# Attention B of a fused encoder block: 64-column values products in pairs of array halves, row sums by ones products

## The reference

```python
def mla_attention(c_q, c_kv, k_rope, pos, g_cq, g_ckv, w_uq, w_ukv, g_q, g_k):
    q = (rms_norm(c_q, g_cq) @ w_uq).reshape(Bn, S, B_HEADS, B_QK_DIM)      # 8 heads of 96
    kv = (rms_norm(c_kv, g_ckv) @ w_ukv).reshape(Bn, S, B_HEADS, B_NOPE_DIM + B_V_DIM)   # 64 + 64
    ...
    def block(args):
        qi, i = args
        q_chunk = (i * Q_BLOCK + jnp.arange(Q_BLOCK)) // CHUNK              # chunks of 64
        s = jnp.einsum('bqhd,bkhd->bhqk', qi, k).astype(jnp.float32) * scale
        s = jnp.where(key_chunk[None, :] <= q_chunk[:, None], s, -jnp.inf)
        p = jax.nn.softmax(s, axis=-1).astype(v.dtype)
        return jnp.einsum('bhqk,bkhd->bqhd', p, v)
...
merged = gt[:, :, 0] * (y_a @ w_branch_a[l]) + gt[:, :, 1] * (y_b @ w_branch_b[l])
x = x + merged @ w_out[l]
```

## Time and profile before

| | |
|---|---|
| median of 3 runs | 1389.64 us (1389.06 to 1390.81) |
| the profiled execution | 1389.89 us |
| its span | 1388.1 us |
| TensorE busy | 1363.3 us, 98% |
| VectorE busy | 813.6 us, 59% |
| GpSimd busy | 760.2 us, 55% |
| ScalarE busy | 407.4 us, 29% |
| attention B, first slot to last | 172.20 us |

### The profile page before, as it was taken

How to read it: one execution, slowest core, us unless ns; L and a number is a source line. 1 busy time by engine, 2 the same in 40 slices (tenths; PEclk the granted TensorE clock), 3 DMA queues, 4 the chain that set the end, 5 groups by cost and what they waited for, 6 DMA issues and landing times.

```text
span 1388.1 us, 17597 instructions
## 1 busy us (share of the span) xinstructions
PE 1363.3 (98%) x6644; PEld 1117.4 (80%) x6644; DVE 813.6 (59%) x1422; ACT 407.4 (29%) x857; POOL 760.2 (55%) x618
## 2 busy tenths in 40 slices
PE   8999999999999999999999999999999999999998
PEld 8999887668867766888887888888888888888887
DVE  5401725643577762455256667677667777666776
ACT  5113235642355654000033212221221221221121
POOL 2341924445384520354308666668766667866697
PEclk9999999999999999999999999999999999999999
DMA  7120231211120002735101112211111221111113
GB/s 238 41 61 16 86 97 61 65 62 46 41 46 16 9 16 62 246 93 208 33 26 51 53 39 61 61 50 42 54 53 46 61 62 38 54 54 51 48 46 122
DMA packets 102885, 90.82 MB, mean 65 GB/s; under 512 B 21905, under 2 KB 84881, under 8 KB 102801
## 3 DMA queue, kind: packets, MB, share of 16 engines
q1 hardware_dynamic: 102656, 89.17, 21.2%
q10 hardware_dynamic: 144, 0.52, 0.1%
HBM read 76.99 MB, written 12.62 MB: 65 GB/s over the span
## 4 chain that ended last, share of the span: by engine, by line
PE 88%; POOL 4%; DVE 3%; DMA 2%; issue 1%; ACT 1%; ACTq 0%; POOLq 0%; DVEq 0%
PE PS L1452 76%; PE PS L1651 3%; PE PS L1459 2%; PE PS L1826 1%; PE PS L1546 1%; PE PS L1548 1%; DMA r_row<-r_store 1%; PE PS L1631 1%; PE PS L1615 1%; PE PS L1632 1%; PE PS L1633 1%; POOL gw_lo L928 1%; POOL scA L991 1%; POOL b_rstd L879 1%; PE PS L1568 1%
## 5 line engine op out<-in xcount | busy, mean ns | idle before, releaser
L2229 DVE TENSOR_TENSOR xr<-PS,xr 128x512 f32<-128x512 f32 x240 | 161.6, 684 | 80.5 <-PE PS L1452 80.5
L2229 DVE TENSOR_TENSOR sum<-PS,sum 128x512 f32<-128x512 f32 x168 | 114.2, 687 | 90.8 <-PE PS L1452 90.8
L1452 PE MATMUL PS<-w_hi,u_hi 128*128 128x512 f32 x420 | 163.6, 390 | 1.0 <-DVE u_lo L2233 1.0
L1452 PE MATMUL PS<-w_lo,u_hi 128*128 128x512 f32 x420 | 163.4, 389 | 0.0
L1452 PE MATMUL PS<-w_hi,u_lo 128*128 128x512 f32 x420 | 163.4, 389 | 0.0
L1058 POOL TENSOR_TENSOR w_lo<-w_raw,w_hi 128x512 fp32r<-128x512 f32 x109 | 156.0, 1431 | 9.1
L1452 PE MATMUL PS<-mT_hi,w_hi 128*128 128x512 f32 x512 | 160.4, 389 | 0.0
L1452 PE MATMUL PS<-mT_hi,w_lo 128*128 128x512 f32 x512 | 160.2, 389 | 0.0
L1452 PE MATMUL PS<-mT_lo,w_hi 128*128 128x512 f32 x512 | 160.2, 389 | 0.0
L1387 ACT ACTIVATE relu_t<-PS 128x512 f32<-128x512 f32 x64 | 38.3, 599 | 296.1 <-PE PS L1452 293.2
L870 POOL TENSOR_SCALAR w_hi<-w_raw 128x1024 fp32r<-128x1024 f32 x32 | 38.7, 1209 | 156.0 <-DMA w_raw<-in_w_ff 156.0
(11 more groups left out here) (237 smaller groups left out, 2961.0 us busy)
## 6 DMA issues: line engine op xcount, KB each, us to landing
w_raw<-in_w_ff SPq DMA_DIRECT2D x32, 512.0 KB, 4.1
w_raw<-in_w_ff SPq DMA_DIRECT2D x64, 256.0 KB, 2.6
g_raw<-in_w_in SPq DMA_DIRECT2D x16, 512.0 KB, 3.9
gate_store<-gate SPq DMA_DIRECT2D x16, 512.0 KB, 2.6
x_in<-in_x SPq DMA_DIRECT2D x8, 512.0 KB, 10.3
gate_a<-gate_store SPq DMA_DIRECT2D x8, 512.0 KB, 7.6
gate_b<-gate_store SPq DMA_DIRECT2D x8, 512.0 KB, 4.7
raw<-in_w_out SPq DMA_DIRECT2D x8, 512.0 KB, 3.6
```

Source lines behind the costliest of these rows:

```text
L1452: ins = pe.matmul(o, st, cut(mv), start=first and n == 0, stop=last and n == 2)
L2229: dve.tensor_tensor(out, part, out, ALU.add).then_inc(acc_done, 1)
```

## The change

**Values.** Tiles are taken in groups of four: `values_group(j)` stands in slot 4j + 5, in the place where one tile's product stood. A head has three groups: part 0 (triangle of the first half), part 1 (full tiles), part 2 (triangle of the second half). `vB` has only the 64 value columns. In each group some tiles go to the head's own 64 rows of bank 5 or 6 (`head_rows`), the others to the other 64 rows (`other_rows`): in part 1 tiles 1 and 3 to the own ones, in the triangles tiles 1 and 2. ScalarE copies the other rows to `y_raw` (`y_out`), VectorE adds the own rows from PSUM (`y_add`). `p_set` has 3 x 4 tiles, `y_raw` four tiles of full width.

**Sums.** The sums of a head come from four tiles: `p_sum[0]` or `p_sum[3]` (the first triangle added up by GpSimd, `sums_first`), `p_sum[1]` and `p_sum[2]` (two full tiles each, added by VectorE, `full_add`), and `p_set[2][0]` (the second triangle, by GpSimd in place, `sums_last`). Four products with a weight of 32 columns of ones (`sums(h)`) put them in rows 0, 32, 64 and 96 of bank 6, in slot 7 of the next head; for head 7 in bank 7, behind branch 0. ScalarE copies the bank (`sums_out`), four DMAs move the rows (`sum_move`), VectorE adds three of them and takes both reciprocals, and store, two spreads, `y_norm`, `y_high` and `y_low` follow for both halves at once, `y_norm` 31 and 32 slots behind the head's first.

**Order elsewhere.** `yA_lanes` moves to heads 5 and 6, `branch_splits` 0 to 3 to heads 6 and 7, `branch_load` 0 to 3 from head 1 to head 5. New waits: a part 1 group waits for `sums_out` of the previous head (`s_read`), exp of a new set of four for the group, the additions or the ones products that read it.

```diff
-        p_diag = [place(f"p_diag{i}", 40 + 2 * i, [P, HALF]) for i in range(Q_BLOCK)]
-        p_full = [place(f"p_full{i}", 48 + 2 * i, [P, HALF]) for i in range(P_RING)]
-        y_raw = [place(f"y_raw{i}", 58 + 2 * i, [P, HALF]) for i in range(2)]
+        p_set = [[place(f"p_set{g}_{i}", 40 + 8 * g + 2 * i, [P, HALF]) for i in range(Q_BLOCK)] for g in range(3)]
+        y_raw = [place(f"y_raw{j}", (92, 132, 201.75, 144.75)[j], [P, S]) for j in range(4)]
...
-            def sum_move(u):
-                sp.wait_ge(y_raw_ready, u + 1)
-                sp.dma_start(b_sum[:, u % 2, :], sum_row(u).rearrange("o (p t) -> o p t", t=Q_BLOCK)
-                             ).then_inc(sum_landed[u % 2], 16)
+            def sum_move(h):
+                sp.wait_ge(s_read, h + 1)
+                if h:
+                    sp.wait_ge(rsum_b_ready, h)
+                for part in range(4):
+                    sp.dma_start(b_sum[:, part, :], s_raw[32 * part:32 * part + 1, :].rearrange(
+                        "o (p t) -> o p t", t=Q_BLOCK)).then_inc(sum_landed, 16)
...
+                if h >= 2:
+                    reciprocal_store(h - 2)
                 if more:
-                    nmax_move(h + 1, 0, 1, 2)
+                    nmax_move(h + 1, 0, 1)
+                if h >= 2:
+                    reciprocal_spread(h - 2)
+                if more:
+                    nmax_move(h + 1, 2, 3, 4, 5, 6)
                 if h:
-                    sum_move(2 * h - 1)
...
+                    sum_move(h - 1)
                 if more:
                     nmax_move(h + 1, 7)
...
             for d in range(3):
                 fetch_a(d)
-            sum_move(BLOCKS - 1)
-            reciprocal_store(BLOCKS - 1)
-            reciprocal_spread(BLOCKS - 1)
+            reciprocal_store(B_HEADS - 2)
+            reciprocal_spread(B_HEADS - 2)
+            sum_move(B_HEADS - 1)
+            reciprocal_store(B_HEADS - 1)
+            reciprocal_spread(B_HEADS - 1)
             fetch_a(3)
...
+            def sums_first(h):
+                p, d = p_set[0], first_sum(h)
+                pool.wait_ge(p_ready, HEAD_SLOTS * h + Q_BLOCK)
+                if h >= 2:
+                    pool.wait_ge(s_done, h - 1)
+                pool.tensor_scalar(d[:, 0:P], p[0][:, 0:P], 1.0, 1.0, ALU.mult, ALU.mult).then_inc(sum_step, 1)
+                pool.tensor_tensor(d[:, P:], p[0][:, P:], p[1][:, P:], ALU.add).then_inc(sum_step, 1)
+                for i in (2, 3):
+                    add_step(h, i, d[:, i * P:], d[:, i * P:], p[i][:, i * P:])
...
+            for h in range(1, B_HEADS):
+                sums_last(h - 1)
+                sums_first(h)
+                if h in (1, 3):
+                    chain(h + 3)
+                    chain(h + 4)
...
             y_out(BLOCKS - 1)
+            y_high(BLOCKS - 4)
+            y_high(BLOCKS - 3)
+            sums_out(B_HEADS - 1)
             y_high(BLOCKS - 2)
             y_high(BLOCKS - 1)
...
+            def values_group(j):
+
+                h, part = j // 3, j % 3
+                half = min(part, 1)
                 u, g = 2 * h + half, h // B_GROUP
...
+                pe.wait_ge(p_ready, Q_BLOCK * (j + 1))
+                if part < 2 and u >= 2:
+                    pe.wait_ge(y_added, u - 1)
+                if part == 1 and h:
+                    pe.wait_ge(s_read, h)
...
+                for i in range(Q_BLOCK):
+                    own = (i % 2, i in (1, 2))[part != 1]
+                    c0 = P * i if part != 1 else 0
+                    rows = head_rows(h) if own else other_rows(h)
+                    ins = pe.matmul(PS[rows, 5 + half, c0:HALF], vB[g % 3][:, i + Q_BLOCK * (part == 2), h % B_GROUP, :],
+                                    p_set[part][i][:, c0:HALF], start=part < 2 and i < 2, stop=part != 1 and i >= 2)
+                ins.then_inc(group_done, 1)
+
+            def sums(h):
+
+                bank = sums_bank(h)
+                pe.wait_ge(sum_step, SUM_STEPS * (h + 1))
+                pe.wait_ge(full_added, 2 * (h + 1))
...
+                for i, p in enumerate((first_sum(h), p_sum[1], p_sum[2], p_set[2][0])):
+                    ins = pe.matmul(PS[32 * i:32 * i + 32, bank, :], ones_w[:, :], p[:, :], start=True, stop=True)
+                ins.then_inc(s_done, 1)
...
-                if t >= 2:
-                    values_t(t - 2)
+                if t > Q_BLOCK and t % Q_BLOCK == 1:
+                    values_group(t // Q_BLOCK - 1)
                 a = chunk_at(t)
                 if a is not None:
                     approx(a)
+                if t > HEAD_SLOTS and t % HEAD_SLOTS == SUM_AT:
+                    sums(t // HEAD_SLOTS - 1)
...
+            def full_add(h, i):
+                p = p_set[1]
+                dve.wait_ge(p_ready, HEAD_SLOTS * h + 2 * Q_BLOCK)
+                if h:
+                    dve.wait_ge(s_done, h)
+                dve.tensor_tensor(p_sum[1 + i][:, :], p[2 * i][:, :], p[2 * i + 1][:, :], ALU.add).then_inc(full_added, 1)
...
+            def y_add(u):
...
+                c = 0 if half else P
+                y = y_raw[h // 2][head_rows(h), y_cols(half, c)]
+                dve.wait_ge(y_copied, u + 1)
+                dve.tensor_tensor(y, PS[head_rows(h), 5 + half, c:HALF], y, ALU.add).then_inc(y_added, 1)
...
+            y_add(BLOCKS - 1)
+            sum_reciprocal(B_HEADS - 2)
+            y_norm(BLOCKS - 4)
+            y_norm(BLOCKS - 3)
+            y_low(BLOCKS - 4)
+            y_low(BLOCKS - 3)
+            sum_reciprocal(B_HEADS - 1)
             y_norm(BLOCKS - 2)
-            sum_reciprocal(BLOCKS - 1)
+            y_norm(BLOCKS - 1)
             y_low(BLOCKS - 2)
-            y_norm(BLOCKS - 1)
             y_low(BLOCKS - 1)
```

286 lines of the change are left out of this document (159 added, 127 removed).

## The result

The changed kernel takes 1421.16 us as the median of 4 runs (1417.82 to 1423.16), against 1389.87 before: 1.022 times as long, 95% interval 1.0208 to 1.0232. That is 31 us slower, far outside the range of 1384 to 1400. The profiled execution took 1423.11 us. Executions of the changed kernel differ among themselves as their granted clock does: the one of 1417.82 us shows 0.992 over its whole span, those of 1423.1 show 0.986, the kernel before 0.999.

The account below looks back on a forecast made before the run. TensorE, busy 166.15 of attention B's 172.20 us, was taken as the bound over most of it. Stage -4.5 and end +7.6 make +3.1; 1389.89 + 3.1 - 0.25 is about 1393 us, range 1384 to 1400.

Parts of the forecast that it names:

- Side by side, and the shape: TensorE in attention B: array halves run concurrently, values -31.1, sums +6.9, changes of shape +9.3, in all -14.9 us.
- Rival D: Column halves don't run side by side because both write one bank; 1425 us, chance 0.04.
- No term below is a term of the clock: Granted clock of 1.00 in attention B's windows, so the forecast included no clock term.
- The new waits: Each head's full group waits for ScalarE's copy of the previous sums, 0.5 to 1.2 us per head.
- Lanes and branch splits at 0: On GpSimd, lanes and branch splits move from one idle time to another, costing 0 us.
- VectorE and GpSimd in heads 2 and 4: VectorE busy 20.4 to 21.1 us; GpSimd's gapless chain delays ones products 1.1 to 1.5 us each; gain at most 1.
- Rival E: GpSimd and VectorE additions of SBUF tiles hold each other up; stage +3, end +9, 1401.6 us, chance 0.09.
- The row-max transfer: SP's four sum moves precede the last row-max transfer; second-half scores in fast heads wait 0.5 to 1 us.
- The end: Behind attention B, a longer sum chain and late weights delay branch 4, +7.6 us, bounds +4 and +9.5.
- The spreads of head 7: At the end, transfers spreading head 7's reciprocals, taken at 5.2 us and landed by T + 25.1.
- head 6's store: At the end, store issued at T + 2.1 behind three gate transfers, landed about T + 7.
- 10.4 are held back: Part of TensorE's -14.9 us not reaching the stage, which was forecast to gain only 4.5.

Follow-up runs that it names:

- before_with_pauses: The kernel before, with TensorE made to wait three times for dummy GpSimd operations in heads 6 and 7; 1396.49 us.
- copy_first: The changed kernel with ScalarE's copy of the previous head's sums directly behind exp in slot 8; 1410.75 us.
- norm_early: The changed kernel with y_norm, y_high and y_low two slots earlier, the copy of the sums unmoved; 1422.70 us.
- pairs: copy_first with two values products in every odd slot instead of four in every fourth; 1421.54 us.
- end_order: copy_first with head 7's sums copied before head 6's roundings and branch B's first weight load ahead of head 7's store and spreads; 1403.22 us.
- small_additions: The changed kernel with VectorE's two full-tile additions and their ones products on 64 of 512 columns, most second-half sums incomplete; 1413.80 us.

## Why the prediction was wrong

**Side by side, and the shape: right.** TensorE's work was to fall to 166.2 - 14.9 = 151.3 us; without the clock's share it is 152.4. The switch costs the 0.24 us read from the earlier trace rows. Rival D is out.

**"No term below is a term of the clock": the step that failed.** The stage was to gain 4.5 us and lost 25.0, and 15.5 of the difference are a term that the sum did not have. It was read from windows of the kernel before, in which the clock was 1.00 because TensorE never paused long: 0.16 us at the earlier trace rows, 6 us idle in the whole stage, 1.1 at most at once. A change that takes work from the engine that bounds makes pauses, and these have a price that no row of before showed. In its place stand 15.5 us. That pauses are what brings them is shown by before_with_pauses (3.5 us of clock for a pause of 3.04) and fits copy_first (5.2). The clock's share doesn't follow the sum of idle time, though: norm_early has less idle time than the changed kernel and a larger share (20.4), pairs has 6 us less than copy_first and 18.6.

**The new waits: the second step that failed; right mechanism, mis-sized.** The wait for the copy of the sums was put at 0.5 to 1.2 us a head; it was 2.0 on average and 3.6 at most. The sum took exp, y_high and the copy by their durations, as if ScalarE could start each at once. But y_high waits for y_norm, and VectorE comes late to that (heads 2 to 4) or stands there for a row that waits for SP's queue (heads 5 and 7); the reads of preparations and y_out stand ahead of the copy as well. Copying ahead of all but exp gave 10.4 us, a slot earlier still 4.3 to 5.7.

**Lanes and branch splits at 0: wrong in part.** The branch splits cost GpSimd nothing that shows, as said, but their four loads, moved to head 5, stand 2.24 us ahead of the store of the reciprocals on SP, and the store takes 5.5 us beside them instead of 1.6: this is how the longest pause of the stage begins. I had counted the splits and not the queue. No run has the loads elsewhere, so that what they cost is not shown.

**VectorE and GpSimd in heads 2 and 4: not the bound.** VectorE was to be busy 20.4 to 21.1 us there; it was 17.75 and 19.59 of 23.90 and 26.88. In head 2 one y_low and one kT_lo fall into the next head's window, and a y_norm takes 0.67 us instead of the 0.89 of before. It is late slot by slot all the same: row maxima make TensorE wait 6.4 us (0.3 before). GpSimd's chain costs 3.5 (2.0 before); the ones products wait for its last addition once, 0.8 us, where 1.1 to 1.5 were forecast in each of heads 2 and 4. Rival E named a contention that isn't in the added work to speak of: the additions took 0.68 on average (see below for another).

**The row-max transfer:** forecast 0.5 to 1 us for the fast heads, measured once, 2.4 us, in head 7.

**The end: right, mis-sized.** +7.6 was forecast, +4.8 measured, by the wait that was named, for the weights of branch 4. The spreads of head 7, taken at 5.2 us, landed 3.7 us after their issue; everything ahead was 1.5 to 2 us early too. One step came out by luck: head 6's store, issued at T + 2.1, was taken as landed at T + 7 beside a row of 7.1 us, which would give T + 9.2; SP goes on behind it at T + 6.3 (578.44). With end_order nearly all of it goes.

**The balance.** Forecast: -14.9, of which 10.4 are held back, and +7.6. Measured: -13.8 of work, +23.2 of idle time, +15.5 of clock, +4.8 at the end. The 10.4 held back would have been 17.9 with every wait at its upper end; the idle time that was added is 23.2, more than twice the one and 1.3 times the other. The clock put two thirds as much on top of it.

## What to carry to other kernels

Work taken from the engine that is the bound is worth something only if all that feeds it is ahead by as much; where it isn't, the engine pauses, and on TensorE a pause can cost more than its length: one of 3.04 us was followed here by 3.4 us of lost work and cost 5.2 us in all. When a step is put behind others in an engine's fixed order, follow what these others wait for, through every queue down to SP, before you price the step by its own duration. When batches replace single products, look at the shortest slot between them, not at the mean.

## What the runs showed that was not expected

Clock: a pause of 3.04 us was followed by 6.8 us at the lower level, pauses of 1.15 and 1.14 us by none; but two of 1.44 and 0.97 us within 3 us, in pairs, by some 20 us of it, with TensorE busy from 532 on. Nor does the same wait always do the same: the changed kernel waits 2.00 us for GpSimd in head 0 and then shows 0.58, 0.50, 0.50 and 0.72 in windows of 2 us from 398 on, small_additions waits 1.99 us at the same place and stays at 1.00. What decides between these is left open, and so a part of each difference between two single executions is chance.

Contention: y_norm, in SBUF with two inputs, took 1.62 us in head 6 beside GpSimd's yA_lanes, which the change had moved there, and 0.67 at 547.32, when that step had ended (timelines of DVE and POOL):

```profile
545.18 1.62 DVE L2200 TENSOR_TENSOR y_raw<-y_raw,r_row 64x512 f32<-64x512 f32 x1
...
547.32 0.67 DVE L2200 TENSOR_TENSOR y_raw<-y_raw,r_row 64x512 f32<-64x512 f32 x1
```

```profile
543.87 2.38 POOL L1024 TENSOR_TENSOR yT_lo<-yTa,yT_hi 128x1024 fp32r<-128x1024 f32 x1
```

It cost nothing there: y_norm ended at 546.80, and ScalarE came to y_high only behind exp, at 547.02.
